# The last down projection of a two-layer decoder trunk, ordered tile by tile

## The reference

```python
h = layer_norm(DEEPNORM_ALPHA * h + mix, ln1_g[i], ln1_b[i])
h = layer_norm(DEEPNORM_ALPHA * h + sqrelu_mlp(h, w_up[i], w_down[i]), ln2_g[i], ln2_b[i])
gate = sigmoid(h @ ple_w_gate[i] + ple_b_gate[i])
h = h + gate * (p[i] @ ple_w_proj[i])
```

## Time and profile before

| | |
|---|---|
| median of 3 runs | 3253.4 us (3247.75 to 3253.92) |
| the profiled execution | 3248.94 us, span of its slowest core (core 5) 3247.1 us |
| spans of the 8 cores | 3213.3 to 3247.1 us |
| busy on core 5 | PE 95%, DVE 45%, ACT 51%, POOL 27% |
| HBM traffic over the span | 200 GB/s |

### The profile page before, as it was taken

How to read it: one execution, slowest core, us unless ns; L and a number is a source line. 1 busy time by engine, 2 the same in 40 slices (tenths; PEclk the granted TensorE clock), 3 DMA queues, 4 the chain that set the end, 5 groups by cost and what they waited for, 6 DMA issues and landing times.

```text
span 3247.1 us, 46641 instructions; the slowest of 8 cores (3213.3 to 3247.1 us)
## 1 busy us (share of the span) xinstructions
PE 3081.9 (95%) x15776; PEld 1446.8 (45%) x15776; DVE 1475.4 (45%) x2583; ACT 1658.3 (51%) x2936; POOL 881.8 (27%) x551
## 2 busy tenths in 40 slices
PE   5989986899999999999999999999999999999998
PEld 2444443444444444444444444444444444444443
DVE  3460163625354555446443354556424455445614
ACT  3476044654556455544555545555564645655452
POOL 0240051314133242424213142232312224142402
PEclk9999998999999999999999999999999999999999
DMA  8749959578986465563635544463644644344441
GB/s 201 166 109 180 173 166 216 171 169 199 258 208 210 152 195 184 161 228 143 221 126 192 205 143 166 143 185 111 207 177 148 199 152 178 130 147 158 143 172 65
DMA packets 84760, 556.65 MB, mean 171 GB/s; under 512 B 9680, under 2 KB 9936, under 8 KB 27600
## 3 DMA queue, kind: packets, MB, share of 16 engines
q1 hardware_dynamic: 74304, 485.31, 42.7%
q0 software_dynamic: 10224, 68.36, 14.8%
HBM read 564.83 MB, written 85.46 MB: 200 GB/s over the span
## 4 chain that ended last, share of the span: by engine, by line
PE 82%; DMA 7%; DVE 6%; issue 3%; ACT 2%; SPq 0%; DVEq 0%; ACTq 0%; POOLq 0%
PE ps L725 31%; PE ps L1134 24%; PE ps L732 13%; PE ps L1167 6%; DMA mring<-ws 3%; PE ps L1067 2%; DMA xT<-xs 1%; PE ps L1176 1%; PE ps L763 1%; PE ps L1047 1%; DVE ar L751 1%; DVE h L787 1%; DMA h<-x 1%; DMA sring<-wsb 1%; PE ps L1027 1%
## 5 line engine op out<-in xcount | busy, mean ns | idle before, releaser
L725 PE MATMUL ps<-xT,mring 128*128 128x512 bf16 x4096 | 916.3, 381 | 14.2 <-DVE xT L773 5.7
L1134 PE MATMUL ps<-mring,ar 128*128 128x512 bf16 x4096 | 922.2, 379 | 5.2 <-DMA mring<-ws 3.1
L725 PEld LDWEIGHTS ps<-xT,mring 128*128 128x128 bf16 x4096 | 393.7, 98 | 491.3 <-issue 45.2
L1134 PEld LDWEIGHTS ps<-mring,ar 128*128 128x128 bf16 x4096 | 392.6, 98 | 466.9 <-issue 21.5
L781 POOL TENSOR_TENSOR h<-h,lnr_sb 128x1024 f32<-128x1024 f32 x128 | 306.9, 2401 | 853.2 <-ACT rstd L745 432.4
L732 PE MATMUL ps<-sring,xT 128*128 128x512 bf16 x2048 | 469.0, 386 | 6.7 <-DMA sring<-wsb 5.8
L1119 ACT ACTIVATE tmpa<-ps 128x512 f32<-128x512 f32 x512 | 304.7, 596 | 268.6 <-PE ps L725 266.5
L787 DVE SCALAR_TENSOR_TENSOR h<-h,ps 128x512 f32<-128x512 f32 x256 | 173.8, 681 | 566.5 <-PE ps L1134 512.5
L732 PEld LDWEIGHTS ps<-sring,xT 128*128 128x128 bf16 x2048 | 202.0, 100 | 255.7 <-issue 31.1
L782 POOL TENSOR_TENSOR h<-h,lnr_sb 128x1024 f32<-128x1024 f32 x128 | 305.0, 2389 | 12.7 <-POOL h L781 0.4
L1120 ACT ACTIVATE ar<-tmpa 128x512 bf16<-128x512 f32 x456 | 287.2, 630 | 40.8 <-ACT tmpa L1119 1.5
(11 more groups left out here) (139 smaller groups left out, 2750.5 us busy)
## 6 DMA issues: line engine op xcount, KB each, us to landing
mring<-wsb SPq DMA_DIRECT2D x224, 1024.0 KB, 5.7
sring<-wsb SPq DMA_DIRECT2D x116, 1024.0 KB, 6.1
lnr_sb<-lnr SPq DMA_DIRECT2D x32, 1024.0 KB, 5.9
wsb<-ws POOLq DMA_DIRECT2D x23, 1024.0 KB, 17.5
h<-x SPq DMA_DIRECT2D x32, 512.0 KB, 9.1
mring<-ws POOLq DMA_DIRECT2D x16, 1024.0 KB, 20.8
wsb<-mring SPq DMA_DIRECT2D x16, 1024.0 KB, 20.2
y<-h SPq DMA_DIRECT2D x32, 512.0 KB, 6.3
```

The source lines that it names most:

```text
L725: ins = h.matmul(ps[b.i][:], lhsT=wt[:, (m * 8 + kc) * 128:(m * 8 + kc + 1) * 128], rhs=xT[c][:, kc, :], start=(kc == 0), stop=(kc == 7))
L1134: ins = h.matmul(ps[b.i][:], lhsT=hid(kk)[:, t * 128:(t + 1) * 128], rhs=wt[:, kc * 512:(kc + 1) * 512], start=(kk == 0), stop=(kk == 31))
```

## The change

In the last job alone, the second half of the down projection goes tile by tile with all four units held; each tile's residual add and statistics follow it. In `post` of that job each tile's norm is followed by its own 8 transposes into one bank and 8 moves of 128x128 with scale and shift (planned at 0.3 us on ACT or 0.2 on DVE), in place of 8 moves of 128x512 for all tiles. The scale and shift of the float32 rows (L781, L782) may go to POOL (planned at 2.45) or to DVE (planned at 1.6). The other 15 jobs take the old path.

```diff
+        def ln_tile(c, t, col, base):
+            xa, xr = xnb(c, base, t)
+            b = Bank()
+            def f(h):
+                for kc in range(8):
+                    ins = h.transpose(psb[b.i][:, kc * 128:(kc + 1) * 128], xa[:, kc * 128:(kc + 1) * 128], identb[:])
+                return ins
+            yield mmul(b, xr + ["identb"], 0.45, f)
+            for kc in range(8):
...
+                fa = lambda h, ...: h.activation(out=xT[c][:, kc, ts], in_=psb[b.i][:, cs], func=AF.Identity, scale=g_ap, bias=b_ap)
+                fv = lambda h, ...: h.tensor_scalar(out=xT[c][:, kc, ts], in0=psb[b.i][:, cs], scalar1=g_ap, scalar2=b_ap, op0=ALU.mult, op1=ALU.add)
+                yield either([("act", fa, 0.3), ("dve", fv, 0.2)], [b, "small"], xn(c, [t], [kc]), drop=[b] if kc == 7 else ())
-        def ln_residual(c, i):
+        def ln_residual(c, i, last=False):
...
+                if last:
+                    yield O("act", ... func=AF.Identity, scale=rstd, bias=nmr ..., 1.24)
+                    for a, op in ((0, ALU.mult), (1, ALU.add)):
+                        fr = lambda h, t=t, a=a, op=op: h.tensor_tensor(out=h_tok[c][:, t, :], in0=h_tok[c][:, t, :], in1=lnr[:, a, :], op=op)
+                        yield either([("pool", fr, 2.45), ("dve", fr, 1.6)], hn(c, t) + ["lnr"], hn(c, t))
+                    continue
...
+                if half == 1 and j == NJ - 1:
+                    held = []
+                    for uu in range(4):
+                        held.append((yield from want(RM, layer, U["dn"] + 4 + uu, j)))
+                    for t in range(NT):
+                        for uu in range(4):
...
+                            o = O("pe", f, [wres] + an(uu * 8, 8, [t]), [banks[t]], 1.73, fill=[banks[t]] if uu == 0 else ())
+                            o.rank = MLP
+                            yield o
+                        yield residual_add(c, t, half, banks[t])
+                        yield from ln_stats(c, t)
+                    return
...
             for t in range(NT):
                 yield from ln_norm(c, t, X_LN2)
-            yield from ln_transpose(c, SM_LNC + layer * 32 + 16, X_LN2)
-            yield from ln_residual(c, li)
+                if last:
+                    yield from ln_tile(c, t, SM_LNC + layer * 32 + 16, X_LN2)
+            if not last:
+                yield from ln_transpose(c, SM_LNC + layer * 32 + 16, X_LN2)
+            yield from ln_residual(c, li, last)
```

More of the change, by code:

```diff
@@ L774, in ln_transpose @@
                     yield either([("act", fa, 0.75), ("dve", fv, 0.55)], [b, "small"], xn(c, kcs=[kc]), drop=[b] if i % 2 == 1 else ())
-        def ln_residual(c, i):
+        def ln_tile(c, t, col, base):
[7 more added lines that the diff above has]
+            for kc in range(8):
+                g_ap = small[:, col + kc:col + kc + 1]
+                b_ap = small[:, col + 8 + kc:col + 8 + kc + 1]
+                cs = slice(kc * 128, (kc + 1) * 128)
+                ts = slice(t * 128, (t + 1) * 128)
+                fa = lambda h, kc=kc, cs=cs, g_ap=g_ap, b_ap=b_ap: h.activation(out=xT[c][:, kc, ts], in_=psb[b.i][:, cs], func=AF.Identity, scale=g_ap, bias=b_ap)
+                fv = lambda h, kc=kc, cs=cs, g_ap=g_ap, b_ap=b_ap: h.tensor_scalar(out=xT[c][:, kc, ts], in0=psb[b.i][:, cs], scalar1=g_ap, scalar2=b_ap, op0=ALU.mult, op1=ALU.add)
+                yield either([("act", fa, 0.3), ("dve", fv, 0.2)], [b, "small"], xn(c, [t], [kc]), drop=[b] if kc == 7 else ())
+        def ln_residual(c, i, last=False):
             yield Until(lambda: state["lnr"] > i)
             for t in range(NT):
+                if last:
+                    yield O("act", lambda h, t=t: h.activation(out=h_tok[c][:, t, :], in_=h_tok[c][:, t, :], func=AF.Identity, scale=rstd[c][:, t:t + 1], bias=nmr[c][:, t:t + 1]),
+                            hn(c, t) + [f"rstd{c}_{t}", f"nmr{c}_{t}"], hn(c, t), 1.24)
+                    for a, op in ((0, ALU.mult), (1, ALU.add)):
+                        fr = lambda h, t=t, a=a, op=op: h.tensor_tensor(out=h_tok[c][:, t, :], in0=h_tok[c][:, t, :], in1=lnr[:, a, :], op=op)
+                        yield either([("pool", fr, 2.45), ("dve", fr, 1.6)], hn(c, t) + ["lnr"], hn(c, t))
+                    continue
                 yield O("act", lambda h, t=t: h.activation(out=h_tok[c][:, t, :], in_=h_tok[c][:, t, :], func=AF.Identity, scale=rstd[c][:, t:t + 1], bias=nmr[c][:, t:t + 1]),
@@ L1125, in mlp, with f @@
                 banks = [Bank() for t in range(NT)]
+                if half == 1 and j == NJ - 1:
[4 more added lines that the diff above has]
+                        for uu in range(4):
+                            k, wt, wres = held[uu]
+                            def f(h, b=banks[t], uu=uu, t=t, wt=wt):
+                                for kc in range(8):
+                                    kk = uu * 8 + kc
+                                    ins = h.matmul(ps[b.i][:], lhsT=hid(kk)[:, t * 128:(t + 1) * 128], rhs=wt[:, kc * 512:(kc + 1) * 512], start=(kk == 0), stop=(kk == 31))
+                                return ins
+                            o = O("pe", f, [wres] + an(uu * 8, 8, [t]), [banks[t]], 1.73, fill=[banks[t]] if uu == 0 else ())
[4 more added lines that the diff above has]
+                    return
                 for uu in range(4):
@@ L1149, in post @@
             U = UNITS[layer]
+            last = j == NJ - 1
             for t in range(NT):
                 yield from ln_norm(c, t, X_LN2)
-            yield from ln_transpose(c, SM_LNC + layer * 32 + 16, X_LN2)
-            yield from ln_residual(c, li)
+                if last:
[3 more added lines that the diff above has]
+            yield from ln_residual(c, li, last)
             w2 = []
```

## The result

The changed kernel took 3238.69 us (median of 7 runs, 3237.96 to 3244.23), the kernel before 3250.72 in runs beside it (3247.75 to 3253.92): ratio 0.997, 95% interval 0.9959 to 0.9981 (the two medians alone stand 12.0 apart). Timed again later, the medians are 3239.2 against 3248.6, ratio 0.9971 (0.9961 to 0.9982). In this second set one run of the changed kernel and three of the kernel before fell in a slower state of the chip and are left out. By the first ratio it is faster by 9.8 us (0.3% of 3250.72), with an interval of 6 to 13.

A forecast was written before the change was run, and what follows sets the result against it. PE without a gap to the last down projection (second half starts at T), then waits on norms and DVE; 5.0 + 1.2 + 1.9 - 1.0 + 0.6 = 7.7 us gain, 3253.4 - 7.7 = 3245.7 us, range 3239 to 3252.5.

The forecast's parts named there:

- The order of the down projection: Last down projection: tile by tile, two units of tile 1 pulled forward; norms 0 and 1 near T + 22.6.
- The moves of 128x128: Moves behind each tile's transposes: 0.26 us on DVE, 0.36 on ACT start to start, eight split evenly between both.
- The tail behind the moves: Last job's chain from norms and moves through first tanh, 5.0 us earlier, to DVE's end at 3236.4.
- the tanh stands behind all moves: On ACT before the gates: tanh counts as late for its table, so first tanh comes 3222.8 to 3223.4.
- Rows on DVE: Scale and shift of the last job's float32 rows: 1.2 us each on DVE, up to 3.4 beside POOL.
- The slower rival: DVE's row operations each wait for POOL, up to 3.4 us instead of 1.2; 3 us slower, 3257; chance 0.07.
- The fourth unit: Weight load for the last down projection's second half: lands before the first tile needs it, cost 0.
- PE and DVE at the end: Last gates: PE ends near 3228; DVE, with 16 operations and 4 bias adds behind the first tanh, ends at 3236.4.
- The term of 1.0 for a row operation behind the first tanh: DVE's final stretch: one row operation of tile 3 falls in between, taking 1.0 us from the gain.

The follow-up runs named there:

- e5: The change with each tile's four units forced to stand behind the tile before; tail 88.6 us against 83.6 for the change and 90.6 before.
- e8: The change with the last job's tanh not counted late for its table, placed behind the last exponential; tail 81.0 us against 83.6 for the change.
- e1: The change without its third part, so the rows' scale and shift stay on POOL; tail 82.7 us against 83.6 for the change.
- e2: The kernel before with only the last job's row scale and shift allowed on DVE or POOL; tail 92.6 us against 90.6 before.
- e10: The change with the last job's gate bias added by a PE matmul instead of on DVE; tail 85.1 us against 83.6 for the change.

## Why the prediction was right or wrong

The sign, the size (7.7 against 7.0 in the trace) and the place of the gain were right. The way there was not: two steps failed in opposite directions, and that the size came out near is in part luck. In e5, with the order that I reckoned with, the same change gains 2.0 and not 7.7.

- **The order of the down projection** failed. I had the planner work tile by tile, with two units of tile 1 pulled forward for the load. It makes pairs throughout: a unit that adds into the bank of the unit before counts as ready 0.17 us later than PE is free, so the other tile's unit wins. Tile 3's first unit is then the tenth and not the thirteenth, and norms 0 and 1 started at T + 17.4, not T + 22.6. e5 forces my order and measures its worth: 5.0 us less than the pairs.
- **The moves of 128x128** had the right prices (0.34 on DVE; 5.00/14 = 0.36 from start to start on ACT) and the wrong arrangement. I let ACT and DVE share each tile. The planner orders the readers of one bank, and all 8 moves of a tile read one bank, so they follow one another: tiles 0 and 1 took 5.4 us, not 2.8. With the pairs' 5 us of head start most of it was hidden; in my order it would not have been. The Trainium skill (PSUM — Partial Sum Buffer, section Terms) has it that two engines on one bank and quadrant at once are an error, reads against reads included. I had not weighed that rule; no run here tried it, all are serial on a bank.
- **The tail behind the moves.** Norm 3 began at T + 33.2, 1.7 earlier than forecast: tile 2's multiply went behind nmr 3, not ahead. But tile 2's last five moves went behind norm 3 on ACT, and the 12 moves ended at T + 40.0. First tanh over at T + 41.9 (forecast 41.0), DVE at T + 54.7 (forecast 54.0).
- **That the tanh stands behind all moves** was right, and e8 shows what it costs: 2.6 us, the most of what was tried one by one.
- **Rows on DVE** cost 1.22 alone, as forecast (1.2). The first pair ran undisturbed (2.36 together) and one other waited (1.50). I had 4 to 5 on DVE; there are 7, and with them the planner keeps 28 moves on ACT. I did not see that this part loses: 0.9 of the 7.9 (e1), and 2.0 by itself (e2). The slower rival's mechanism is real, it is only smaller here, since POOL has one operation left.
- **The fourth unit** cost nothing, as forecast.
- **PE and DVE at the end.** DVE sets the end, with four bias adds behind the first tanh, as forecast; PE was at its end 5 us before. The term of 1.0 for a row operation behind the first tanh was empty: DVE's rows ended at 3224.5, ahead of it. Taken apart at the end of the first tanh, the 7.0 are 4.1 ahead of it (forecast 5.0) and 2.9 behind it (forecast 2.7).

## What to carry to other kernels

A part of a change can be a loss inside a gain; take it apart before keeping it. Where a planner orders the work, its small constants (a delay of 0.17 us, a table counted late, who may read a bank, which operation gives a bank back) decide as much as the edit does, and they are worked out from its rules, not from the name of the change. Measure an end effect from a common point in the trace: the tail is the same within 0.2 us over the cores here in most kernels, where whole runs scatter by 6.

## What the runs showed of the hardware

- DVE operations with two inputs in SBUF and POOL operations hold each other up to about the length of an operation: two of L1226 took 3.98 instead of 1.28, two row operations 4.46 instead of 2.36, POOL's 3.18 to 3.26 instead of 2.34. A DVE operation with one such input (L751 in the kernel before) took 2.53 beside POOL instead of 0.81.
- Behind a 3.5 us gap of PE (e10) the first gate took 3.29 to 3.62 us instead of 1.89 in six of eight cores, and as long with a wait inside in the other two; the second was slow in five of them (2.35 to 2.57) and at full pace in three, whose tails are 1.1 shorter. Behind a gap of 2.18 us (the change) the next two gates ran at full pace in three cores (3.62 us) and slower in five (up to 5.30).
